# A conditioned decoder trunk: the sums of its modulation vectors move from full-array matmuls on split weights to four column tiles and a block transpose

## What is computed

```python
e = silu(c @ cond_w + cond_b)                        # one vector of 1024
mod = (e @ ada_w[i] + ada_b[i]).reshape(3, 3, 1024)  # ada_w[i] is 1024 x 9216
shift, scale, gate = mod[:, 0], mod[:, 1], 1 + mod[:, 2]
h = rms_norm(x, g) * (1 + scale) + shift
x = x + 0.5 * gate * ((silu(h @ w1) * (h @ w3)) @ w2)   # an FFN; the mixers are modulated alike
```

## Time and profile before

| | |
|---|---|
| three runs | 2105.23 us median, 2102.99 to 2106.54 |
| profiled execution | 2103.05 us, its span 2101.3 us |
| mean granted clock of PE | 0.98 |
| PE busy | 2043.3 us (97%), 9512 matmul records |
| DVE, ACT, POOL busy | 1113.2, 677.2, 183.8 us |
| memory traffic | 261.80 MB, mean 125 GB/s |

### The profile page before, as it was taken

The page is one execution under the profiler, slowest core; times in us unless marked ns, Lnnn a source line. Parts: engine busy times, 40 slices in busy tenths (PEclk is TensorE's granted clock), DMA queues, the critical chain, the costliest instruction groups (busy, mean ns, idle before and its releaser), DMA issues.

```text
span 2101.3 us, 24264 instructions
## 1 busy us (share of the span) xinstructions
PE 2043.3 (97%) x9512; PEld 1654.3 (79%) x9512; DVE 1113.2 (53%) x1326; ACT 677.2 (32%) x760; POOL 183.8 (9%) x129
## 2 busy tenths in 40 slices
PE   5999999989999999999999999999999999999999
PEld 5888888766567888888788888887787777888887
DVE  7555553588977555533655433364446855333322
ACT  2423232241244232222423222242136744222211
POOL 1100000111302000001100000110001110000000
PEclk9999999999989999999999999999978999999999
DMA  8445443334413444432354422232200032222222
GB/s 326 177 162 197 185 170 143 143 108 138 133 67 125 184 190 180 169 117 98 118 189 189 160 88 84 97 103 99 80 1 1 1 120 81 100 100 91 78 96 95
DMA packets 45414, 261.80 MB, mean 125 GB/s; under 512 B 6416, under 2 KB 7056, under 8 KB 20528
## 3 DMA queue, kind: packets, MB, share of 16 engines
q1 hardware_dynamic: 42288, 256.84, 33.3%
q10 hardware_dynamic: 3072, 4.23, 0.8%
HBM read 250.49 MB, written 2.10 MB: 120 GB/s over the span
## 4 chain that ended last, share of the span: by engine, by line
PE 85%; DVE 6%; DMA 3%; issue 3%; ACT 2%; POOL 1%; SPq 0%; DVEq 0%; POOLq 0%; ACTq 0%
PE ps L1323 25%; PE ps L1325 25%; PE ps L1324 25%; PE ps L1664 3%; DVE w L811 1%; DMA raw<-down_d 1%; PE ps L1344 1%; PE ps L1546 1%; DMA stage<-ada_d 1%; PE ps L1678 1%; DVE act_tmp L824 1%; DVE ada_acc L824 1%; PE ps L1584 1%; ACT w L560 1%; PE ps L1437 1%
## 5 line engine op out<-in xcount | busy, mean ns | idle before, releaser
L1323 PE MATMUL ps<-h_hi,w 128*128 128x512 f32 x1648 | 649.9, 394 | 8.2 <-DVE w L976 6.8
L1325 PE MATMUL ps<-h_hi,w 128*128 128x512 f32 x1648 | 648.9, 394 | 0.0
L1324 PE MATMUL ps<-h_lo,w 128*128 128x512 f32 x1648 | 646.2, 392 | 0.0
L1323 PEld LDWEIGHTS ps<-h_hi,w 128*128 128x128 f32 x1648 | 310.4, 188 | 84.6 <-DVE w L976 8.1
L1324 PEld LDWEIGHTS ps<-h_lo,w 128*128 128x128 f32 x1648 | 310.4, 188 | 68.6
L1325 PEld LDWEIGHTS ps<-h_hi,w 128*128 128x128 f32 x1648 | 310.5, 188 | 66.5
L811 DVE TENSOR_TENSOR w<-raw,w 128x1408 fp32r<-128x1408 f32 (+1 forms) x100 | 186.4, 1864 | 239.3 <-ACT w L560 239.2
L560 ACT ACTIVATE w<-raw 128x1408 fp32r<-128x1408 f32 (+1 forms) x100 | 157.0, 1570 | 443.9 <-PE ps L1325 377.0
L1323 PE MATMUL ps<-g_hi,w 128*128 128x512 f32 x704 | 274.6, 390 | 4.3 <-DVE w L811 4.3
L1324 PE MATMUL ps<-g_lo,w 128*128 128x512 f32 x704 | 273.9, 389 | 0.0
L1325 PE MATMUL ps<-g_hi,w 128*128 128x512 f32 x704 | 273.9, 389 | 0.0
(11 more groups left out here) (210 smaller groups left out, 1925.3 us busy)
## 6 DMA issues: line engine op xcount, KB each, us to landing
raw<-up_d SPq DMA_DIRECT2D x88, 1024.0 KB, 6.3
ada_raw<-ada_d SPq DMA_DIRECT2D x64, 1024.0 KB, 4.8
raw<-down_d SPq DMA_DIRECT2D x64, 704.0 KB, 4.1
raw<-mix_d SPq DMA_DIRECT2D x28, 1024.0 KB, 4.8
stage<-ada_d SPq DMA_DIRECT2D x12, 1024.0 KB, 13.0
u_blk<-u SPq DMA_DIRECT2D x64, 64.5 KB, 2.1
u_blk<-u ACTq DMA_DIRECT2D x64, 64.5 KB, 2.1
x<-x_t_d SPq DMA_DIRECT2D x2, 1024.0 KB, 18.0
```

What stands on the lines that cost most here:

```text
L1323: pe.matmul(dst, a_hi_, b_hi_, start=start, stop=False, skip_group_check=True)
L1324: pe.matmul(dst, a_hi_, b_lo_, start=False, stop=False, skip_group_check=True)
L1325: return pe.matmul(dst, a_lo_, b_hi_, start=False, stop=stop, skip_group_check=True)
```

## The change

All 32 later blocks take one new form, and the split with its copies goes. The ones become the weights (128x32, f32) and `ada_acc` the moving operand: four f32 matmuls, the b-th on column tile b of the array, into partitions 32b to 32b+31. Its 128 columns are four runs of 32 taken from `ada_acc` with a stride of 128. All 32 rows of a tile come out equal. DVE then transposes the 128x128 result in PSUM in blocks of 32x32 into `ada_t`, and the first column of each block holds the sums in the layout of `mods`. `ada_take` has to wait until the transpose is done (`ada_col`) before it adds the bias. In the loop ACT's copy (L611) and the POOL subtraction (L478) go away, and PE waits for DVE's `ada_step` instead of POOL's `accl_done`. ACT's two loops over the up steps become one.

```diff
@@ buffers
-        acc_hi, acc_lo = parts[:, 0, :], parts[:, 1, :]
+        ada_rows = ps[:, 7, 0:P].rearrange("p (n r) -> p n r", n=4)
+        ada_t = ps[:, 7, P:2 * P]
@@ POOL
-            def acc_lows(j, n):
-                with pool.Fori(0, n) as i:
-                    pool.wait_ge(acch_done, i + (N_SPLIT[j] + 1))
-                    pool.tensor_tensor(acc_lo, ada_acc[:, :], f32(acc_hi), ALU.subtract).then_inc(accl_done, 1)
@@ ACT, up_step
-                if ada and s == 0:
-                    act.wait_ge(ada_step, 8 * (Q_FFN[j] + i) + (STEP0 - 48))
-                    act.activation(acc_hi, ada_acc[:, :], ACT.Copy).then_inc(acch_done, 1)
@@ DVE, ada_take
+                if not isinstance(q, int) or q >= 6:
+                    dve.transpose(ada_t, ps[:, 7, 0:P]).then_inc(ada_col, 1)
+                    dve.wait_ge(ada_col, q - 5)
+                    dve.tensor_tensor(dst, ada_t.rearrange("p (n r) -> p n r", n=4)[:, :, 0], b, ALU.add) \
+                        .then_inc(mod_done, 1)
+                    return
@@ PE
-            def ada_reduce(q, acc):
+            def ada_reduce(q):
                 pe.wait_ge(ada_step, 8 * q + (STEP0 - 40))
-                for c in range(4):
-                    last = pe.matmul(ada_ps[:, 2 * c:2 * c + 1], acc[:, c * P:(c + 1) * P], ones[:, 0:1], start=True, stop=True)
-                last.then_inc(ada_sum, 1)
-            def ada_reduce_split(n):
-                pe.wait_ge(accl_done, n)
-                for c in range(4):
-                    at = slice(c * P, (c + 1) * P)
-                    pe.matmul(ada_ps[:, 2 * c:2 * c + 2], acc_hi[:, at], ones_r[:, 0:2], start=True, stop=False)
-                    last = pe.matmul(ada_ps[:, 2 * c:2 * c + 2], acc_lo[:, at], ones_r[:, 0:2], start=False, stop=True)
+                for b in range(4):
+                    last = pe.matmul(ada_rows[32 * b:32 * b + 32, :, :], ones[:, 0:32],
+                                     ada_acc[:, :].rearrange("p (n b r) -> p n b r", n=4, b=4)[:, :, b, :],
+                                     start=True, stop=True, skip_group_check=True)
                 last.then_inc(ada_sum, 1)
@@ PE, up_step
-                reduce_ = (lambda: ada_reduce_split(N_SPLIT[j] + i)) if ada and s == 1 else None
+                reduce_ = (lambda: ada_reduce(Q_FFN[j] + i - 1)) if ada and s == 1 else None
```

More of the change, by code:

```diff
@@ L81 @@
 Q_BODIES = [11, 11, 7, 0]
-N_SPLIT = [0, 10, 20]
 Q_DOWN = 17
@@ L210, in trunk @@
         start_pe = sem("start_pe")
-        acch_done = sem("acch_done")
-        accl_done = sem("accl_done")
+        ada_col = sem("ada_col")
         ada_sum = sem("ada_sum")
@@ L482, in _ @@
             h_odds(0)
-            acc_lows(0, 10)
             for c in range(KD):
@@ L532, in _ @@
                 h_odds(m)
-                if m < 5:
-                    acc_lows(m - 2, min(Q_BODIES[m - 2], 10))
             def split_low(c):
@@ L604, in h_his, with up_step @@
                         act.activation(h_hi[:, c, :], t_buf(c), ACT.Identity, bias=shift).then_inc(hhi_done, 1)
-            def up_step(j, i, s, split=True, ada=False, first=None):
+            def up_step(j, i, s, split=True, first=None):
                 n = N_UP[j] + 2 * i + s
-                if ada and s == 0:
-                    act.wait_ge(ada_step, 8 * (Q_FFN[j] + i) + (STEP0 - 48))
-                    act.activation(acc_hi, ada_acc[:, :], ACT.Copy).then_inc(acch_done, 1)
                 tmp = act_tmp[:, s, :]
@@ L630, in ffn @@
                     up_step(j, 0, s, first=FFN_ENTRY[j] if s == 0 else None)
[L631 to L638, removed]
+                with act.Fori(1, 10) as i:
+                    for s in range(2):
+                        up_step(j, i, s)
                 for s in range(2):
-                    up_step(j, 10, s, split=False, ada=(nb == 11))
+                    up_step(j, 10, s, split=False)
                     hi(N_DOWN[j] + s, DOWN)
@@ L1500, in ffn @@
                     if j == 0:
-                        ada_reduce(Q_DOWN - 1 + i, ada_acc)
+                        ada_reduce(Q_DOWN - 1 + i)
                 if j and nb == 11:
-                    ada_reduce(Q_FFN[j] + 10, ada_acc)
+                    ada_reduce(Q_FFN[j] + 10)
             pe.wait_ge(ones_done, 3)
```

## The result

| | before | after |
|---|---|---|
| median of the runs | 2105.23 us (7 runs, 2102.99 to 2108.84) | 2090.85 us (7 runs, 2079.45 to 2095.95) |
| ratio after / before | | 0.9927, 95% interval 0.9909 to 0.9946 |
| profiled execution, its span | 2103.05, 2101.3 us | 2091.65, 2089.9 us |
| mean granted clock of that execution | 0.983 | 0.984 |
| PE busy | 2043.3 us | 2029.9 us |

The kernel became faster, by 14.4 us in the medians where 10.2 were forecast. A second set of six runs of the same kernel had its median at 2093.35, inside it. The forecast of 2095.0 was 4.1 us too high by the first set and 1.7 by the second. On which side of the bound a set of six or seven runs falls is partly chance: single runs of this kernel spread over 16.5 us.

The account below looks back on a forecast made before the run. PE was taken to bound the kernel, except in FFN 0's down stage. Blocks 10.2 plus POOL wait 0.95 less transposes 0.9 made 10.2 us, from 2105.23 to 2095.0 us; range 2091.5 to 2101.8 us.

Parts of the forecast that it names:

- What bounds it: PE, busy without waits in the up stages; in FFN 0's down stage a loop of weight loads, ACT and DVE.
- The block, 0.89 to 0.54 us: Each later modulation reduction on PE: 0.89 us now, 0.54 us in the new form, saving 0.35 us.
- the taps' pace: Convolution tap matmuls, same tiles and type, run four column tiles side by side, taking the time of one.
- the switch of 0.32: PE leaving the full array and coming back, per block: 0.32 us, of which 0.09 at the entry.
- POOL's wait, 0.95 us: At the start of the second FFN, PE's wait for POOL's subtraction goes, saving 0.95 us.
- Where the saving counts, 29 of 32: 27 up-stage blocks and those at 434 and 1015 us count, 10.2 us; three in the down stage give nothing.
- The transposes in the loop, 0.9 us: Three DVE takes in FFN 0's down stage each gain a 0.3 us transpose: cost 0.9 us, bounds 0.45 to 2.1.
- In the loop there is no cover: In FFN 0's down stage no DVE idle time hides the transposes; three takes lie on the loop.
- The sum, 10.2 us: Whole kernel: 10.2 from blocks, plus 0.95 for POOL, less 0.9 for transposes, gives 10.2 us less.
- first rival: Tiles don't keep the convolution taps' speed: a block saves about 0.15 us, 4.4 us less, 2100.8 us; chance 0.13.
- second out: Second rival: the four tiles run in turn, 1.20 us a block, 8.9 us more, 2114.1 us; chance 0.06.
- third out: Third rival: saving eaten elsewhere, up stages meeting a loop of their own; time as before, 2105; chance 0.03.

Follow-up runs that it names:

- loads_before: Kernel before, with each ada load in FFN 0's down stage issued one loop turn later, behind two more weight loads: median 2100.75 us, ratio 0.9974.
- one_tile: Changed kernel with all four matmuls of a block on column tile 0, three quarters of the later sums left out: median 2110.47 us, ratio 1.0032.
- tiles_with_split: Kernel before with the new four-tile blocks and transpose, ACT copies and POOL subtractions still made and waited for: median 2091.25 us, ratio 0.9938.
- plain_all: Changed kernel with the old full-array f32 blocks in all 32 places, no transpose, no split copies: median 2104.11 us, ratio 0.9995.
- after_again: The changed kernel unedited, measured again against the kernel before on the same chip: median 2093.35 us, ratio 0.9938.
- filler: Changed kernel with three small unused full-array matmuls behind every block, padding it to the old cost: median 2104.82 us, ratio 0.9998.
- filler_early: Changed kernel with nine small unused matmuls ahead of each of ten blocks in FFN 0's up stage: median 2100.42 us, ratio 0.9974.
- filler_late: Changed kernel with 90 small unused matmuls in the last FFN's up stage, behind the attention stage: median 2100.82 us, ratio 0.9983.
- two_transposes: Changed kernel with a second DVE transpose, result unused, in each later ada_take: median 2091.02 us, ratio 0.9927.

## Why the prediction came out as it did

- **What bounds it:** right. PE without waits in the up stages, a loop outside PE in the down stage of FFN 0. loads_before, which empties that loop, turns its waits into time and confirms the second half.
- **The block, 0.89 to 0.54 us:** right; 0.56 was measured, and 0.34 saved instead of 0.35. The parts held: two rounds at the taps' pace, with 0.02 us more for the first, and the switch of 0.32. one_tile has the same 0.02 behind its first record (0.133 us to the second, 0.109 between the later ones). The Trainium skill, "TensorEngine Tiling (Array Packing)", Key Properties, says that altering the tiling mode drains the engine. The trace agrees in that the switch costs something: here 0.09 us on the way in and the rest on the way out, 0.32 of the 0.56 us. By the other rule, in the Trainium skill, "TensorE: Matmul & The Clock Gate", part 3, loads overlap matmuls in flight only where the row group differs (its text on the mechanism also allows a background weight buffer). The trace disagrees with the "only": four loads of 32 columns on the same rows vanish between rounds 0.13 us apart (exposed, all eight would have made the block 0.76).
- **POOL's wait, 0.95 us:** right for the profiled execution, where it is gone. It is no constant, though: it depends on when DVE's sum is ready, and tiles_with_split, which still has it, shows 0.14 us. The times of plain_all can't tell 0.95 us from nothing.
- **Where the saving counts, 29 of 32:** right. In after_again PE's waits in the loop grew by 1.0 us, three times 0.34. (The trace of after alone, with 0.9, hides a half-clock stretch in the same stage.)
- **The transposes in the loop, 0.9 us:** a step that failed, and it pushed the forecast up. 0.32 us each was right, but their cost in the loop was nothing. The step is "In the loop there is no cover": the 1.37 us of the first `ada_acc` step were read as work, when the up stage has the same instruction at 0.5 us. The cover is POOL's sum of squares, to whose end this step is tied in every trace, within 0.29 us.
- **The sum, 10.2 us:** its corrected form is 29 x 0.34 + 0.95 - 0 = 10.8 us. The two profiled executions differ by 10.4 without their clock; the two sets of runs differ from before by 10.8 and 9.6 at equal clock. The measurement can't tell 10.2 from 10.8, and the error in the transposes alone stays well inside the range.
- **The step that failed, and took the result out of the range: PE's clock, put at nothing without a reason.** The sum goes from the median of before to 2095.0 as if the time at half clock stayed what it was, and the range has no term for it; for the scatter of the runs it takes 2.2 us from three runs of before. Yet the half-clock stretches were in the page's row of granted clock. The runs showed in its place that the mean clock rose from 0.9823 to 0.9845 over the 13 runs of after. 0.0022 is 4.0 us at 1.80 us for each 0.001 (standard error 1.3), and this is what lies between the forecast and 2090.85; for the seven runs of that set alone it is 4.6 us. The rise itself is clear of noise. Its cause stays open: filler, filler_early and filler_late point to the distance between the later stages, but each by differences that chance makes once in twenty cases. That one set fell outside the range and the next inside is the luck of the draw.
- **The rivals:** the tiles keep the taps' pace (first rival out). They run side by side (second out, and one_tile shows that its price was right). No stage ate the saving (third out).

## What to carry to other kernels

Price a small matmul block as entry, rounds and exit, each from a place where the same tile and type already run; here that came within 0.02 us of the measured block. Look at what an instruction costs elsewhere before you call its duration work: a first step of 1.4 us that takes 0.5 in another stage is held by something, here by POOL's work beside it, and then has room ahead of it. And in a kernel whose PE drops to the lower clock somewhere, compare runs at equal clock first, and give the range of the forecast a few microseconds for it: a change that touches none of that code can still come with another mean clock, as this one did, whatever the cause.

## What had not been expected of the hardware

- The same code at the start of the attention stage ran at half clock for 41.0, 37.5, 27.3 (two_transposes) or 17.1 us (tiles_with_split, filler_late). That is not a property of the kernel alone: the changed kernel itself had 37.5 us in one execution and 41.0 in the other. What the kernel moves is the mean over its runs: 0.9817 to 0.9829 where FFN 1 and 2 take as long as before, and 0.9840 to 0.9849 where they take 0.34 us a block less. one_tile, whose blocks take longer, had 0.9838, so it is not simply "shorter is better".
- In the traces of the down stage DVE and POOL hold each other up. A DVE step took 1441 ns beside POOL's sum and 478 ns where POOL was silent; an instruction put ahead of it ran for nothing, twice (1085, 883 ns), and the end of the step stayed 0.28 to 0.29 us behind POOL's. POOL's own add takes 1.92 to 2.22 us there, where the same line takes as little as 1.27 us elsewhere, and ends 1.13 to 1.16 us after DVE's low part. It is not the load: in loads_before, where the weights and `ada_raw` come in another order and PE waits for nothing, the step still has 1443 ns. A kernel with that sum on another engine was not run.
- A DVE instruction that waits for the one ahead of it started 0.27 us after its end inside a loop (117.42 to 117.69), where two register instructions stand between, and 0.03 us outside (370.42 to 370.45).
